# Modulation, norm and the first Q, K and V projection in one block instead of two

## The reference, cut to what matters

```python
s_c, s_cc = jax.nn.silu(c), jax.nn.silu(c_ctx)
mod = s_c @ w_ada[0] + b_ada[0]              # latents; mod_c the same from s_cc for the context
shift, scale = mod[:, None, :D], mod[:, None, D:2 * D]
u_lat = _rmsnorm(h_lat, norm_g[0]) * (1.0 + scale) + shift
u_ctx = _rmsnorm(h_ctx, norm_g[0]) * (1.0 + mod_c[D:2 * D]) + mod_c[:D]
z = u_lat @ w_in                             # 8 parts of 1024 columns; Q, K, V, a gate, a convolution branch
```

## Time and profile before

| | us |
|---|---|
| median of 3 runs | 2403.7 (2403.24 to 2404.94) |
| the profiled execution's own time | 2403.63 |
| its span in the trace | 2401.8 |
| PE busy | 2261.0 (94%) |
| VectorE, ScalarE, GpSimd busy | 1501.9, 1188.4, 528.3 |
| first projection matmul | 74.45 |
| last copy of V in the prologue | 118.18 |

### The profile page before, as it was taken

One profiled execution on the slowest core, in us unless ns is written; L12 is line 12 of the kernel. 1 busy time (PEld: TensorE's weight loads), 2 busy tenths in 40 slices (PEclk: granted clock), 3 DMA queues, 4 the chain that ended last, 5 costly groups with the idle time before them and its releaser, 6 DMA issues. The chain is left out here.

```text
span 2401.8 us, 33875 instructions
## 1 busy us (share of the span) xinstructions
PE 2261.0 (94%) x12000; PEld 1966.3 (82%) x12000; DVE 1501.9 (63%) x2368; ACT 1188.4 (49%) x1714; POOL 528.3 (22%) x303
## 2 busy tenths in 40 slices
PE   4799999999999999999997999799999999995998
PEld 3688888888888888888885888688998999894887
DVE  5167575774757757576576436557766776667444
ACT  4244434444344443444444334366777678767322
POOL 1333132331322313223230300022212221220300
PEclk8899999999999999999998999899999999997999
DMA  6212211221112211122116555111111111114654
GB/s 247 62 35 68 63 57 33 68 72 59 57 33 73 71 55 57 33 81 63 55 27 226 163 167 175 55 40 53 53 52 54 53 53 58 48 53 140 218 154 144
DMA packets 165352, 199.79 MB, mean 83 GB/s; under 512 B 51064, under 2 KB 125944, under 8 KB 162168
## 3 DMA queue, kind: packets, MB, share of 16 engines
q1 hardware_dynamic: 155304, 174.53, 23.2%
q10 hardware_dynamic: 9792, 23.07, 2.7%
q0 software_dynamic: 144, 0.52, 0.1%
HBM read 166.11 MB, written 31.98 MB: 82 GB/s over the span
## 5 line engine op out<-in xcount | busy, mean ns | idle before, releaser
L950 PE MATMUL ps<-u_hi,w_hi 128*128 128x512 f32 (+1 forms) x1536 | 559.5, 364 | 16.6 <-POOL w_lo L637 16.6
L950 PE MATMUL ps<-u_hi,w_lo 128*128 128x512 f32 (+1 forms) x1536 | 545.2, 355 | 0.0
L950 PE MATMUL ps<-u_lo,w_hi 128*128 128x512 f32 (+1 forms) x1536 | 544.1, 354 | 0.0
L950 PEld LDWEIGHTS ps<-u_hi,w_hi 128*128 128x128 f32 x1536 | 290.6, 189 | 54.1 <-POOL w_lo L637 16.7
L950 PEld LDWEIGHTS ps<-u_hi,w_lo 128*128 128x128 f32 x1536 | 290.3, 189 | 41.9
L950 PEld LDWEIGHTS ps<-u_lo,w_hi 128*128 128x128 f32 x1536 | 291.2, 190 | 37.3
L1525 POOL TENSOR_TENSOR o_w_lo<-o_w_raw,o_w_hi 128x1024 fp32r<-128x1024 f32 x48 | 138.8, 2891 | 669.5 <-ACT o_w_hi L1540 669.5
L1795 PE MATMUL ps<-u_hi,o_w_hi 128*128 128x426 f32 (+2 forms) x640 | 238.0, 372 | 13.9 <-POOL o_w_lo L1525 9.3
L742 ACT ACTIVATE probs<-probs,neg_max 128x640 f32<-128x640 f32 (+1 forms) x160 | 122.8, 768 | 251.5 <-DVE neg_max L858 250.4
L637 POOL TENSOR_TENSOR w_lo<-w_stage,w_hi 128x1024 fp32r<-128x1024 f32 x64 | 153.4, 2397 | 418.6 <-ACT w_hi L695 418.6
L656 POOL TENSOR_TENSOR bias_tile<-bias_piece,col_mask 128x384 f32<-128x384 f32 x128 | 142.7, 1118 | 440.0 <-DVE neg_max L858 439.9
(11 more groups left out here) (176 smaller groups left out, 4274.6 us busy)
## 6 DMA issues: line engine op xcount, KB each, us to landing
y_tile<-y_scratch SPq DMA_DIRECT2D x72, 512.0 KB, 5.1
w_stage<-in_w_even SPq DMA_DIRECT2D x64, 512.0 KB, 3.7
o_w_raw<-in_w_odd SPq DMA_DIRECT2D x48, 512.0 KB, 3.6
ada_piece<-in_w_ada SPq DMA_DIRECT2D x16, 1024.0 KB, 5.7
wout_raw<-in_w_out SPq DMA_DIRECT2D x16, 1024.0 KB, 10.1
ada_pieces<-in_w_ada SPq DMA_DIRECT2D x4, 2048.0 KB, 18.3
y_scratch<-h_backward SPq DMA_DIRECT2D x16, 512.0 KB, 2.7
h_scratch<-h_tile ACTq DMA_DIRECT2D x18, 256.0 KB, 2.3
```

The lines of the kernel that those rows point to most:

```text
L950: last = nc.tensor.matmul(ps[:, bank(j, g), 0:t - f], w[:, slot, c * P:(c + 1) * P], x[:, c, f:t], start=(c == 0 and n == 0), stop=(c == K ...
```

## The change

`mod_and_norm` is gone as a block. Its work stands in `even_layer`'s prologue, in another order:

- SyncE loads ada 0, x pair 0, biases, ada 2, x pair 1, the Q and K weights, ada 1, the V weights (into a buffer of their own), ada 3 in two halves, and then x pairs 2, 3 and 4, the masks and the bias pieces.
- A chunk of one token group is turned into one of three PSUM banks (3, 5, 7). ScalarE reads it there and writes hi with scale and bias applied; VectorE reads it there too and writes the modulated values into one of three small buffers, and then takes lo from it and hi. GpSimd makes no lo of u any more.
- PE takes Q and K chunk by chunk, with the turning three chunks ahead between them, then V, group by group.
- The modulation rows go through one PSUM bank, one after the other, and each is turned as soon as it is copied.
- GpSimd clears `klo` only when all of x is turned, since x lies in that place.

```diff
+            def u_hi(g, c):                                   # ScalarE
+                act.wait_ge(mod_ready, c // 4 + 1)
+                act.wait_ge(x_turned, KC * g + c + 1)
+                nc.scalar.activation(uhi[:, c, f:t], turned_chunk(g, c), ACT.Identity, scale=k["gs"][:, 0, 0, c, st:st + 1],
+                                     bias=k["gs"][:, 0, 1, c, st:st + 1]).then_inc(u_hi_done, 1)
...
+            def prologue():                                   # ScalarE
+                copy_row(0)
+                square(0)
+                square(1)
+                root(0)
+                copy_row(1)
+                square(2)
+                square(3)
+                root(1)
+                split_hi(0, 0)
+                split_hi(0, 1)
+                for c in range(3):
+                    u_hi(0, c)
+                copy_row(2)
+                u_hi(0, 3)
+                act.wait_ge(v_loaded, 16)
+                nc.scalar.activation(v_hi_w[:], v_raw[:], ACT.Copy).then_inc(w_hi, 1)
+                copy_row(3)
+                u_hi(0, 4)
+                u_hi(0, 5)
+                square(4)
+                u_hi(0, 6)
+                square(5)
+                root(2)
+                u_hi(0, 7)
+                square(6)
+                square(7)
+                root(3)
+                copy_first(CQ, 0)
+                copy_first(CK, 0)
+                u_hi(1, 0)
+                u_hi(1, 1)
+                copy_first(CV, 0)
+                u_hi(1, 2)
+                u_hi(1, 3)
+                square(8)
+                u_hi(1, 4)
+                square(9)
+                root(4)
...
+            def modulate(g, c):                               # VectorE
+                dve.wait_ge(u_hi_done, v + 1)
+                if v >= 3:
+                    dve.wait_ge(u_lo_done, v - 2)
+                nc.vector.tensor_scalar(xt[v % 3][:, 0:t - f], turned_chunk(g, c), k["gs"][:, 0, 0, c, st:st + 1],
+                                        k["gs"][:, 0, 1, c, st:st + 1], ALU.mult, ALU.add).then_inc(xt_done, 1)
...
+            def split_chunks(g, c0, c1):
+                modulate(g, c0)
+                for c in range(c0 + 1, c1):
+                    modulate(g, c)
+                    u_low(g, c - 1)
+                u_low(g, c1 - 1)
...
+                scale_rows(0, link)                           # VectorE's prologue
+                mod_half(0, link)
+                scale_rows(1, link)
+                split_chunks(0, 0, 4)
+                mod_half(1, link)
+                split_chunks(0, 4, KC)
+                scale_rows(2, link)
+                scale_rows(3, link)
+                split_chunks(1, 0, 4)
+                scale_rows(4, link)
+                split_chunks(1, 4, KC)
+                split_chunks(2, 0, KC)
...
+                mod_row(0)                                    # PE's prologue
+                mod_columns(0)
+                mod_row(1)
+                mod_columns(1)
+                for c in range(3):
+                    turn_x(0, c)
+                for c in range(4):
+                    first(CQ, 0, c)
+                    first(CK, 0, c)
+                    turn_x(0, c + 3)
+                    if c == 1:
+                        mod_row(2)
+                        mod_columns(2)
+                for c in range(4):
+                    first(CV, 0, c)
+                mod_row(3)
+                mod_columns(3)
+                for c in range(4, KC):
+                    first(CQ, 0, c)
+                    first(CK, 0, c)
+                    if c == 4:
+                        turn_x(0, 7)
+                for c in range(4, KC):
+                    first(CV, 0, c)
+                    if c >= 5:
+                        turn_x(1, c - 5)
+                for c in range(KC):
+                    first(CQ, 1, c)
+                    first(CK, 1, c)
+                    if c + 3 < KC:
+                        turn_x(1, c + 3)
...
             def prologue():                                   # GpSimd
                 split_lo(0, 0)
+                split_lo(1, 1)
                 nc.gpsimd.memset(toe[:], 0.0).then_inc(zeros_set, 1)
-                split_lo(1, 1)
+                pool.wait_ge(w_hi, 3)
+                nc.gpsimd.tensor_tensor(v_lo_w[:], v_raw[:], v_hi_w[:].bitcast(F32), ALU.subtract).then_inc(w_lo, 1)
...
+                pool.wait_ge(x_turned, NG * KC)
                 for h in range(2):
```

More of the change, by code:

```diff
@@ L988, in turn_v @@
             def turn_v(i):
+                pe.wait_ge(bank_free[bank(BG, 0)], half(i, BG, 0))
                 pe.wait_ge(bank_free[bank(BG, 1)], half(i, BG, 1))
@@ new lines, in mod_columns, with turn_x @@
+            def mod_columns(n):
+                j = ADA_ORDER[n]
+                pe.wait_ge(row0_copied, n + 1)
+                for q in range(4):
+                    at = 2 * (4 * j + q)
+                    last = nc.tensor.matmul(ps[:, 6, at:at + 2], rows0[:, j, q * P:(q + 1) * P], k["pick"][:],
+                                            start=True, stop=True)
+                last.then_inc(mod0_turned, 1)
+            def turn_x(g, c):
+                v = KC * g + c
+                if c == 0:
+                    pe.wait_ge(x_scaled, tiles(g)[-1] + 1)
+                if v >= 3:
+                    pe.wait_ge(xt_done, v - 2)
+                for n, t in enumerate(tiles(g)):
+                    last = nc.tensor.transpose(turned_chunk(g, c)[:, n * P:(n + 1) * P], x[:, t, c * P:(c + 1) * P],
+                                               k["ident"][:])
+                last.then_inc(x_turned, 1)
@@ new lines, in _, with first @@
+            FREE = {(CQ, 1): (0, 1), (CK, 1): (1, 1), (CV, 1): (0, 2), (CK, 2): (1, 2), (CQ, 2): (0, 3), (CV, 2): (0, 4)}
+            def first(j, g, c):
+                f, t = EVEN_GROUPS[g]
+                if c == 0:
+                    if g == 0:
+                        pe.wait_ge(w_lo, j - CQ + 1)
+                    else:
+                        pe.wait_ge(bank_free[FREE[j, g][0]], FREE[j, g][1])
+                pe.wait_ge(u_lo_done, KC * g + c + 1)
+                w = slice(c * P, (c + 1) * P)
+                hi, lo = (v_hi_w[:, w], v_lo_w[:, w]) if j == CV else (whi[:, j - CQ, w], wlo[:, j - CQ, w])
+                for n, (wt, u) in enumerate(((hi, uhi), (hi, ulo), (lo, uhi))):
+                    last = nc.tensor.matmul(ps[:, first_bank(j), 0:t - f], wt, u[:, c, f:t],
+                                            start=(c == 0 and n == 0), stop=(c == KC - 1 and n == 2))
+                if c == KC - 1:
+                    last.then_inc(proj, 1)
```

397 lines of the change are left out of this document (175 added, 222 removed).

## The result

The changed kernel took 2407.46 us (median of 20 runs, 2405.52 to 2411.32) against 2404.45 us (20 runs, 2402.27 to 2407.23) of the kernel before: a ratio of 1.0014, 95% interval [1.0008, 1.0020], or 3.4 us longer (2 to 5). The forecast of 2397.5 us was wrong, by 10 us and in sign, and the time lies above its range.

What follows compares the result with a forecast made beforehand. TensorE, busy 2261 of 2401.8 us, was taken as the bound, to be won where it idles. First projection matmul at 35.8, plus 73.2, plus 3.0 for the clock ends V at 112.0, 6.15 earlier: 2397.5 us, range 2387 to 2406.

Steps and rivals of the forecast that it cites:

- First projection matmul at 35.8: Prologue: loads, modulation row, scaling and first turn let TensorE start projecting at 35.8 us instead of 74.45.
- The meeting: Prologue, from about 25 us: GpSimd's Q and K weight splits hold up VectorE's scalings; scaled at 31.7 instead of 27.1.
- mild meeting: Rival: VectorE's scalings slip in ahead of GpSimd, 4.6 us earlier, and the clock stays up: 2389.9 us; chance 0.24.
- Waits 16.9: Between the first projection matmul and V's end, TensorE's waits for other engines sum to 16.9 us.
- The skill's rule: A GpSimd read holds VectorE instructions with two SBUF inputs: u_low(0,3) up to 2.3 us later, sum 0.9 worse, 2398.4.
- V's end at 112.0: End of the prologue's V projection: 109.0 us plus 3.0 for the clock, 6.15 before 118.15.
- The pointer operands: Prologue's u_hi and modulate: taken at 0.6 and 0.69 us from copies, with nothing added for pointers.
- Two falls of the clock: Prologue behind the first matmul: TensorE's clock falls to half twice, at 1.5 us each, 3.0 in all.
- GpSimd's chain ahead of the first body: klo memsets, bias tiles, masking and BG split end 0.5 us after V; cost nothing, with 1.9 to spare.
- every us before 118.15 comes off the span, since nothing behind it is changed: Whole kernel: V's earlier end, 6.15 us, shortens the span in full; later work costs the same.
- the half clock: Rival: TensorE, paced by other engines, stays at half clock from 59.1 us on, 20 us more: 2417.5; chance 0.13.
- loads out of order: Rival: load pieces share the engines, first projection matmul at 53, 17 us later, 6 won back: 2408; chance 0.05.

Runs made afterwards that it cites:

- experiment 4: The changed kernel with GpSimd's first split of the Q and K weights waiting until pair 0 is scaled: 2403.68 us, 0.9997 of the kernel before.
- experiment 7: The changed kernel without scale and bias through pointers (Copy and constants, so modulation is left out): 2403.32 us, 0.9997 of the kernel before.
- experiment 2: The changed kernel with 96 one-column VectorE memsets ahead of the loop of the bodies, moving it to instruction 236: 2405.12 us, 1.0004 of the kernel before.

## Why the prediction was wrong

- **First projection matmul at 35.8: right.** 36.65 and 35.44 in two traces. The meeting was priced at 4.6 us, and without it (experiment 4) the matmul is 4.44 and 3.23 earlier. The rival "mild meeting" fell. That the exclusion also held a 128x2 operation was not foreseen.
- **Waits 16.9: right in size** (17.9), and most places too: chunk 4 of group 0 at 60.76 (59.1), idle 3.6 (3.15); turn(1,0) at 72.62 (69.1); group 1's chunk 4 at 87.83 (83.6).
- **The skill's rule: right.** u_low(0, 2 and 3) at 44.54 took 3.45 us for two, 2.1 more than the 0.68 of each alone, beside GpSimd's split of V's weights. The Trainium skill, SBUF — State Buffer, "Who interferes with whom", states this for a VectorE instruction with two SBUF inputs; the measured time agrees, and 2.1 is near the 2.3 that the forecast read for the operation. Its share of 0.9 in the sum was left out there and isn't measured apart.
- **V's end at 112.0: mis-sized, by 3.7 us.** 0.85 is the first matmul, 1.0 the waits, and 1.9 what TensorE itself took, with the clock (61.2 us against 59.3). The pointer operands, which the forecast had at nothing, bear on the waits: without them V ends 1.5 to 2.3 earlier (experiment 7). Two falls of the clock were counted, for 3.0 us. There were two, but the first stands in the stretch of 42 to 48 us and not before chunk 4 of group 1, whose wait was only 2.43: the number of falls agrees by luck. The half clock after 60.76 lasted 5.2 us, within the 3.2 to 6 us that the forecast read from the earlier trace rows; what a fall cost wasn't measured apart.
- **GpSimd's chain ahead of the first body: at nothing, right.** Its split for BG ends at 115.62, 0.1 before V's last copy (0.5 behind it in the forecast), and BG's first matmul comes at 118.12, 2.4 behind the copy as forecast.
- **The step that failed: "every us before 118.15 comes off the span, since nothing behind it is changed".** Hardly anything behind it is changed in the text, but the instructions ahead of a loop decide where its code lies. That costs 2.4 us over seven bodies against the same kernel with the loop elsewhere (three pairs), 1.5 against the kernel before (without the loads the changed kernel's bodies are 1.0 us shorter than those before; why, no run shows), and 2.6 us of the time in experiment 2. With V's end 2.45 earlier in the profiled pair, or 1.3 earlier as the mean of two traces each, it takes the gain nearly whole.
- **The remaining 3 us: the clock at the hand-over, and whether the change brings that on is open.** 1.3 won and 1.5 lost would be no change; the measured ratio is 3.4 us above. The same sentence of the forecast took the stretch behind the last body at nothing too. In the two traces of each kernel it is 2.4 us longer up to the first `rms` (262.3 against 259.9), with one more fall of the clock behind the same 1.7 us of idle TensorE. That fall is in 8 of the 11 traces with the new prologue, and in none of the 3 with the old one. The work there is the same in both, and 3 of the 11 are without it, so the change doesn't force it; that it makes it likelier, no run shows, and three traces are few. The rest of the 3.4 us is within what single traces differ by.
- The rivals of the half clock (2417.5) and of loads out of order (2408; its own terms give 2408.5) did not happen, though the measured time is next to the second: a number that agrees is no evidence for a mechanism.

## What to carry to other kernels

An edit ahead of a loop can lengthen the loop: compare the instruction queues' packets and the loop's own length, from a mark in the first body to the same mark in the last, before the gain of a prologue is booked. A large idle time on an engine with slack may cost next to nothing while 0.3 us elsewhere does: follow who waits for the result. Compare a trace's own execution with the median of its kernel before a difference of 2 us between two traces is read as one between the kernels. And when a serial chain is broken up into a hand-written order, the order itself can be the largest term: here other orders, and a split moved behind the scaling, turned a loss of 3 us into a gain of 15 to 17 us with the same instructions.

## What the runs showed of the hardware

- VectorE's loop of 344 instructions was served without code loads between 214 and 1181 us when it began 108 instructions past a multiple of 128, and took five loads of 8 KB a body at 12, 28, 60 and 124 past, with 2.70 to 3.07 us of idle VectorE at the start of six bodies.
- While GpSimd runs a TENSOR_TENSOR, VectorE holds back even a 128x2 TENSOR_TENSOR (2.35 instead of 0.16 us). In experiment 4, beside the split of 26.86 to 31.52, two modulates, which read PSUM, took 1.66 us at 28.93, as long as at 34.24 in the changed kernel with no split under way; the lo behind them took 1.55 instead of 0.68.
- With scale and bias through pointers ScalarE takes 777 against 597 ns for 512 columns from PSUM, VectorE 808 against 689.
- Behind the same 1.7 us of idle TensorE, in work that all versions share, the granted clock fell in 8 of 14 traces and stayed up in 6. With the fall the stretch to the first `rms` took 261.3 to 263.7 us, without it 259.7 to 260.7.
